# The bias table's products in place of two products of zeros ahead of the first projection, with their loads first on GpSimd

## The reference, cut to what matters

```python
h = rms_norm(x, norm_mix[l])                 # layer l of the first block
... = split(h @ w_in_l)                      # the "first projection" is the first piece of this, for l = 0

kv  = rms_norm_2(mem, g_mem) @ w_mem_kv      # keys and values of the memory, second block
bias = t5_table[t5_bucket(offs)]             # dilated attention of the second block: a bias for each distance
logits = einsum(q, kgat) * scale + bias
```

## Time and profile before

| what | value |
|---|---|
| median of 3 runs | 1578.17 us (1578.12 to 1578.44) |
| the profiled execution | 1578.25 us |
| its span, first to last instruction | 1575.5 us |
| TensorE busy | 1450.5 us, 92% of the span |
| VectorE, ScalarE busy | 790.1 us, 317.4 us |
| GpSimd busy | 22.7 us |
| moved by DMA | 380.23 MB, 241 GB/s over the span |

### The profile page before, as it was taken

How to read it: one execution, slowest core, us unless ns; L and a number is a source line. 1 busy time by engine, 2 the same in 40 slices (tenths; PEclk the granted TensorE clock), 3 DMA queues, 4 the chain that set the end, 5 groups by cost and what they waited for, 6 DMA issues and landing times.

```text
span 1575.5 us, 20364 instructions
## 1 busy us (share of the span) xinstructions
PE 1450.5 (92%) x8450; PEld 1017.4 (65%) x8450; DVE 790.1 (50%) x1533; ACT 317.4 (20%) x668; POOL 22.7 (1%) x41
## 2 busy tenths in 40 slices
PE   9999999999999999999999999999999577576577
PEld 6798898999445998898998446655544233133132
DVE  4888567756666977658656656534321000001001
ACT  3235430122002226330221002334400000000000
POOL 0000000000000000000000003100000000000000
PEclk9999999999999999999999999999999788788789
DMA  9574334444453534344444456555899999999998
GB/s 337 179 266 161 108 108 160 161 161 162 190 183 101 187 112 157 108 161 161 161 161 161 179 191 204 182 212 197 315 384 426 426 427 427 426 427 427 427 418 315
DMA packets 114925, 380.23 MB, mean 241 GB/s; under 512 B 10836, under 2 KB 23252, under 8 KB 104144
## 3 DMA queue, kind: packets, MB, share of 16 engines
q1 hardware_dynamic: 111952, 369.53, 61.3%
q0 software_dynamic: 2880, 9.36, 1.9%
HBM read 377.25 MB, written 5.73 MB: 243 GB/s over the span
## 4 chain that ended last, share of the span: by engine, by line
PE 79%; DMA 18%; SPq 2%; DVE 1%; issue 0%; ACT 0%; DVEq 0%
DMA ring<-in_w 17%; PE bank L1553 13%; PE bank L1606 12%; PE bank L1379 9%; PE bank L1187 7%; PE bank L1194 6%; PE bank L1303 4%; PE bank L1756 4%; PE bank L1351 3%; PE bank L1327 2%; PE bank L1655 2%; PE bank L1526 1%; PE bank L1528 1%; PE bank L1252 1%; PE bank L1278 1%; SPq L971 1%
## 5 line engine op out<-in xcount | busy, mean ns | idle before, releaser
L1756 PE MATMUL bank<-ring,region 128*32 128x512 f32 x208 | 113.9, 711 | 50.7 <-DMA region<-in_w 50.7
L1756 PE MATMUL bank<-region 128*32 128x512 f32 x512 | 114.1, 709 | 44.8 <-DMA ring<-in_w 44.8
L1606 PE MATMUL bank<-region 128*128 128x512 f32 x320 | 140.6, 592 | 0.0
L1187 PE MATMUL bank<-hT,ring 128*128 128x256 f32 x512 | 115.2, 381 | 0.0
L1606 PEld LDWEIGHTS bank<-region 128*128 128x128 f32 x320 | 60.5, 190 | 74.6 <-issue 74.6
L1187 PEld LDWEIGHTS bank<-hT,ring 128*128 128x128 f32 x512 | 95.5, 190 | 13.6 <-issue 1.0
L1553 PE MATMUL bank<-region 128*128 128x128 f32 x768 | 100.5, 275 | 0.0
L1553 PEld LDWEIGHTS bank<-region 128*128 128x128 f32 x768 | 93.0, 192 | 0.0
L1756 PEld LDWEIGHTS bank<-region 128*32 128x32 f32 x512 | 28.8, 129 | 89.3 <-issue 89.3
L1756 PEld LDWEIGHTS bank<-ring,region 128*32 128x32 f32 x208 | 25.5, 129 | 83.9 <-issue 83.9
L1817 PE MATMUL bank<-region 128*32 128x512 f32 x192 | 60.8, 735 | 17.5 <-DMA hT<-in_w 15.7
(11 more groups left out here) (500 smaller groups left out, 2666.8 us busy)
## 6 DMA issues: line engine op xcount, KB each, us to landing
region<-in_w SPq DMA_DIRECT2D x43, 2048.0 KB, 38.7
ring<-in_w SPq DMA_DIRECT2D x30, 2048.0 KB, 37.8
ring<-in_w_in SPq DMA_DIRECT2D x26, 2048.0 KB, 8.7
ring<-in_w_up SPq DMA_DIRECT2D x16, 2048.0 KB, 8.1
ring<-in_w_down SPq DMA_DIRECT2D x32, 1024.0 KB, 6.3
own_slot<-in_w SPq DMA_DIRECT2D x7, 2048.0 KB, 43.2
ring<-in_w_out SPq DMA_DIRECT2D x6, 2048.0 KB, 7.7
region<-in_w SPq DMA_DIRECT2D x22, 512.0 KB, 8.6
```

The costliest lines, as they stand in the source:

```text
L1187: t = mm(b[:, 0:T], w[:, k, :], act[:, k, :], start=(k == 0), stop=(k == KD - 1))
L1606: t = mm(b[:, :], left[:, t2, :], right[:, t2, :], start=(c4 == 0 and t2 == 0), stop=(c4 == 7 and t2 == 1))
L1756: t = mm(b[32 * e:32 * e + 32, :], xg[:, k, 32 * e:32 * e + 32], four[e][c][:, 512 * (k % 2):512 * (k % 2) + 512], start=(k == 0), stop=(k ...
```

## The change

The three bias products move from the piece "kv" to the place of the two zero products, ahead of the first projection. VectorE's part of them moves to the place right behind `turned_rows` of j = 1 of the first norm. Their banks are given between the two halves of the transposed `x`. GpSimd no longer waits for the second half of `x`, so that the three loads are the first thing that it issues.

```diff
@@ the plan of banks
             if l == 0:
                 give_turns(l, "hT", 0)
+                for g in range(DIL_G):
+                    bk.give((2, "t5", g))
             bk.give((l, "d", 0))
             give_turns(l, "hT", 1)
@@
                     give_turns(2, "memT", 0)
                     give_turns(2, "memT", 1)
-                    for g in range(DIL_G):
-                        bk.give((2, "t5", g))
@@ GpSimd
         def _(pool):
-            pool.wait_ge(x_late_loaded, 16)
             pool.dma_start(t5_onehot, a["c_t5"]).then_inc(t5_loaded, 16)
@@ TensorE
                 if l == 0:
                     turn_half(0, 0)
-                    idle_products(2, 512)
+                    distance_rows()
                 first_rows(N_MIX[l], [(l, "d", i) for i in range(NT)], arrived((l, "d")) if l else slot(0), raw_tile)
@@
                         turn_half(N_MEM, 0)
                         turn_half(N_MEM, 1)
-                        distance_rows()
                         memory_rows(arrived((0, "kv"))[:, :, 0:cols])
@@ VectorE, norm(n)
                     turned_rows(n, j)
-                if n == N_MEM:
-                    distance_rows()
+                    if (n, j) == (0, 1):
+                        distance_rows()
                 dve.wait_ge(ss_ready, n + 1)
```

## The result

Eight executions of the changed kernel took 1577.79 to 1582.97 us, median 1581.20; eight of the kernel before 1576.06 to 1578.44, median 1576.72. The ratio is 1.0021, 95% interval 1.0012 to 1.0030: slower, by about the 0.2% that can be told from no change. Forecast were 1577.1 us, a range from 1576.0 to 1579.4, and no measurable change; the median lies above that range. The times scatter over 5 us now, over 2.4 before.

The account below looks back on a forecast made before the run. TensorE was taken to bound the kernel (79% of the chain that ended last). Start +1.2 and memory -2.3 gave -1.1 us on 1578.25, so 1577.15, forecast as 1577.1 us, range 1576.0 to 1579.4, no measurable change.

Parts of the forecast that it names:

- The path: TensorE bounds the chain from 1.50 us; its gains or losses in the first 41 us reach the end one for one.
- VectorE's 3.2 us: VectorE's six bias instructions leave the memory piece; forecast to gain nothing; a rival counted them: -4.3 us, 1573.9, chance 0.04.
- Place two: At the memory's transposes: bias products leave, `memory_rows` starts earlier, held only by j = 1; gain 2.3 us (2.2 to 2.4).
- Place one: At the start: bias products replace 1.72 us of zero products before the first projection; loss 1.2 us (0.95 to 1.54).
- S: Time the bias products start, after x's first transposes and the three loads' landing; taken as 7.9, between 7.63 and 8.22.
- the forecast's own formula: At the start, the projection begins at S + 2.67 in place of 9.35, so the loss is S - 6.68 us.
- The crowding: At the start, the three loads (217.5 KB) delay x's first half by at most 0.59 us, at least nothing.
- The clock: TensorE's pace at the start: idle for its loads, it could fall to half pace, costing 2.95 us; only in rival D.
- rival D: At the start, late loads (S = 10.1) also drop TensorE's clock: sum +4.05, 1582.3 us, slower; chance 0.05.
- The base: The profiled execution of the kernel before, 1578.25 us with span 1575.5, to which the sum of -1.1 us was added.

Follow-up runs that it names:

- the repeat: The changed kernel run once more, unaltered, against the kernel before: eleven executions from 1577.37 to 1582.63 us, ratio 1.0017.
- the zero products kept: The changed kernel with the two zero products put back between the transposes of x and the bias products; ratio 1.0015 against the kernel before.
- the run with the loads alone: The kernel before, with only GpSimd's wait for the second half of x removed, so its three loads go first; ratio 1.0014.

## Why the prediction was wrong

- **The path: right.** That TensorE hands every microsecond of the start on to the end holds within 0.4 us over 18 traces, and VectorE's 3.2 us counted for nothing.
- **Place two: right.** A gain of 2.3 us was forecast, 2.37 measured; j = 1 alone held `memory_rows` up.
- **Place one: the first step that failed.** S was taken as 7.9, the middle of what a late x could make of it, though the loads' own likely landing, 8.0, gave 8.1, and TensorE waits for the later of the two. It was 8.90: the first issue came 0.53 us later than SP's (1.28), and the third load took 6.4 us in place of 6.1, which puts its landing at 8.85 in place of 8.0. With S = 8.9 the forecast's own formula has the start lose 2.2 us, and a sum of -0.1; measured without the clock's 1.73, the start lost 2.40 and the sum is 0.03. This alone would have left the forecast of no change standing.
- **The crowding: mis-sized.** Bounded by 0.59 us from bytes over rate; alone it moved the projection by 1.47, through the weights that I had not counted, and x itself landed 0.4 to 2.2 us later in the 14 traces with GpSimd's loads first. With S at 8.22 the sum is -0.76, not "below -0.8" as written.
- **The clock: the step that carried the time out of the range.** The sum had nothing for it; it stood in rival D, right in kind, wrong in its condition. I let it decide from S = 9.2 and gave it 0.05. It fell with S between 8.75 and 9.08, in all five traces, and cost 1.73 us in the first and about 1.8 more where it stayed down longer, against 2.95 in D. It doesn't need the idle time that I made its condition: it fell as well behind small tiles without a wait. In the three versions in which nothing but transposes stands ahead of the small tiles it fell in 8 of 9 traces; with zero products ahead of them, or full tiles in their place, in none of 7. Small tiles alone don't do it either: at the old place the same products stand between 37.8 and 40.4, and the stretches of the kernel before show no fall behind them:

```profile
37.80:40.40 2.60, 2.60 (x7) 0.35 (x6) 2.51 (x6) 2.57 (x8) 0.00 (x0) 1.00 1.00 370
40.40:42.00 1.60, 1.60 (x5) 0.85 (x5) 1.53 (x5) 1.44 (x3) 0.00 (x0) 1.00 1.07 367
```

  Ahead of them lie some 30 us at the full pace there (from 7.47 on), and at the start only transposes and zero products, in part at the half pace.
- **The base.** The profiled execution of before was one with a low clock at the router, in the upper of the two groups. 1577.1 was thus an absolute time for such executions.

Over the five traces `memory_rows` starts at 42.95 on average, 2.5 us later than before. The eleven executions of the repeat have a mean of 1580.2 against 1577.7, +2.5, but that is no match: their spans are 3.6 us longer (1578.2 against 1574.6), and 1.1 us come back outside the span. The 1.1 us of span that the traces don't have lie in the executions with spans over 1579.2, of which none was traced, and stay open. That small tiles right behind the start let the clock fall rests on the counts above, with one trace of nine against it and with those executions untraced that took longest with the zero products kept; whether rows or columns of the tile matter, and how much full work ahead of them is enough, wasn't tried.

## What to carry to other kernels

A load that was never urgent becomes part of the critical path when its consumer moves ahead: price its issue, its landing and what it pushes back, each from a row, and put it on a queue whose order you control. Filler that keeps an engine awake has a job of its own; here neither products that waited nor small ones that didn't kept the clock up in every trace. Compare spans as well as times: the four versions here whose mean time is 0.9 to 1.6 us under the kernel before have its mean span to within 0.5 us. Where a trace is one execution of several kinds, look for the place that makes the kinds before you subtract a microsecond from it.

## What was not expected of the hardware

- The granted clock fell behind 2.66 us of products of 32 x 4 tiles that followed one another without a gap (0.50 from 11 to 13 us, two of two), and not behind products of 128 x 128 of the same length (three of three), nor behind the small ones at 38 to 40 us.
- Three loads of 217.5 KB from GpSimd's queue delayed the landing of 512 KB on the other queue from 4.2 to between 4.6 and 6.4 us after its issue, and of the weights behind it from 6.3 to 8.5 us in the run with the loads alone. With the three loads on the same queue, issued behind the 512 KB, these took 4.7, 5.0 and 4.8 us.
- The part of the time outside the span goes with the version: 2.7 to 3.5 us in the three versions that keep the two zero products, 1.8 to 2.3 us in the five that don't.
